# Two stacked transformer blocks with eight experts: the column order of the gate and up products

## The chip, the cores and the metric

The kernel runs on one core of a Trainium2 chip. Its engines work side by side: TensorE multiplies matrices (rows named PE; its loads of the stationary operand are PEld), VectorE (DVE) and ScalarE (ACT) work on elements, GpSimd (POOL) is hardly used, and SyncE (SP) issues most DMA transfers. Data lie in SBUF, 128 partitions wide; TensorE writes its sums to eight banks of PSUM, each with 512 fp32 columns a partition. The metric is device time in microseconds (us) from start to end of one execution, lower is better. Times of single instructions are in nanoseconds (ns).

## What is computed

The reference passes 256 tokens of width 1024 through two blocks. The first has two layers with attention, pooling, a recurrent part and a dense feed-forward part. The second has two layers with convolution and attention; the feed-forward part of its last layer is a mixture of experts. Only that mixture is touched here:

```python
def swiglu(h, w_gate, w_up, w_down):
    return (jax.nn.silu(h @ w_gate) * (h @ w_up)) @ w_down

def moe_swiglu(h, w_router, b_router, w_gate, w_up, w_down):
    ...
    for e in range(N_EXPERTS):          # 8 experts
        out = out + combine[:, e:e + 1] * swiglu(t, w_gate[e], w_up[e], w_down[e])
```

Each token uses its two best experts (`combine` is zero for the others). Gate and up matrices are 1024 x 3584 for each expert, the down matrix is 3584 x 1024, all fp32. All three together are 352 MB, more than half of what the kernel reads.

## The kernel before

**Products in three parts.** An fp32 product is made of rounded parts. ScalarE writes the rounded weights (`whi`, line 1046) from the buffer in which they arrived (`ring`); VectorE subtracts them from the original and writes the rest (`wlo`, in the experts' stage `wlo_moe`, line 1421). For activations the same holds (`xg` is a name of both parts, `xg_hh` and `xg_ht` are the two for the other pair of experts). A product is then hi x hi + hi x lo + lo x hi, three matmuls into the same bank: that is the helper `mm3`, and in the trace all its matmuls of the experts' stage have line 2099. In these matmuls both operands have the type fp32r (rounded). Some small products elsewhere use plain fp32 operands; their stream through TensorE is slower, and the trace shows two records for each such matmul.

**The experts' stage** is written out by hand in `pe_routed`, `act_routed` and `dve_routed`. Tokens of an expert are gathered into 128 places. The loop runs over 56 steps, one for each pair of an expert `e` and a block `f` of 512 of its 3584 hidden columns. A step on TensorE: the gate product (`hidden(n, "gate")`), four transposes of the step before (`turn`, line 2157), the up product, and the down product of the step before. In some steps come small products for gathering and scattering tokens (`gather`, `turn_weights`, `scatter`).

**A gate or up product**: the stationary operand is a 128 x 128 tile of the gathered tokens, the moving operand is a weight tile of 128 x 512, and the result is a whole bank of 128 x 512. Over 8 tiles of the contraction and the three parts this gives 24 matmuls for each. A down product has 24 matmuls too: 4 tiles of the contraction, two banks, three parts, and again 512 moving columns.

**Buffers.** Six slots take the arriving pieces of weights, 1 MB each, six to a step. Each piece is split in two halves of 1024 columns (`HALVES`), for which there are again six places: four in `whi`/`wlo_moe` and two in `EXTRA` (the names `extra_hi`, `extra_lo`). All of them begin at a byte address that is 96 modulo 256 (`WEIGHT_LINE`); the tokens' tiles begin at 32 modulo 256 (`ACT_LINE`). SyncE issues the transfer into a slot when VectorE has read it. Gate products of step n go to bank 0 or 2, up products to bank 1 or 3, from which ScalarE (line 2239, silu) and VectorE (line 2318) read whole rows in the plain order.

Of the kernel before, what the change touches and what calls it, by code (L numbers as in the profile page):

```python
# [124 lines left out]
def build(nc, t, dense=False):  # L125

    with ExitStack() as ctx:
# [55 lines left out]
        def over(name, at, *shape):  # L183
            return nc.alloc_sbuf_tensor_at(name, [128, *shape], F32R, offset=base + 4 * at)
# [5 lines left out]
        XG = [[over(f"xg{i}", 8192 + 2048 * i, 8, 2, 128) for i in range(2)],  # L190
              [nc.alloc_sbuf_tensor_at("xg_hh", [128, 8, 2, 128], F32R, offset=HH_at),
               nc.alloc_sbuf_tensor_at("xg_ht", [128, 8, 2, 128], F32R, offset=hT_at)]]
# [12 lines left out]
        PS = [ctx.enter_context(nc.psum_tensor(f"bank{i}", [128, 512], F32)) for i in range(8)]  # L205
# [1869 lines left out]
        def stage(n):  # L2075

            at = first_moe + 6 * n - (2 if n > 0 else 0)
            up = 2 if n < len(seq) else 0
            return {"gate": range(at, at + up), "up": range(at + up, at + 2 * up),
                    "down": range(at + 2 * up, at + 2 * up + (2 if n > 0 else 0))}  # L2080
# [4 lines left out]
        def pe_routed(pe, tail):  # L2085
# [3 lines left out]
            def take(*name, until):  # L2089
                i = misc[0] % 2  # L2090
                misc[0] += 1
                for signal, *end in misc[1][i]:
                    pe.wait_ge(*signal(*end))
                misc[1][i] = until
                BANK[name] = 6 + i
                return PS[6 + i]

            def mm(out, lhsT, rhs, start, stop):
                return pe.matmul(out, lhsT, rhs, start=start, stop=stop, skip_group_check=True)  # L2099

            def mm3(out, a, b, start, stop):
                mm(out, a[0], b[0], start, False)
                mm(out, a[0], b[1], False, False)
                return mm(out, a[1], b[0], False, stop)

            def half(n, i):
                pe.wait_ge(*(lo_made if n < first_moe + 2 else lambda *x: moe_lo["r"]("lo", *x))(n, i))
                return HALVES[n, i][0:2]

            def gather(p, g, x, bank=None):  # L2110

                until = [(r_vec if x else r_hi, "xg", p, g, x)]
                if bank is None:
                    b = take("xg", p, g, x, until=until)
                else:
                    for signal, *end in tail[bank]:
                        pe.wait_ge(*signal(*end))
                    tail[bank], BANK["xg", p, g, x] = until, bank
                    b = PS[bank]
                pe.wait_ge(*r_vec("select", 2 * p + 1))  # L2120
                for i in range(2):
                    pe.wait_ge(*(v_rout("hnl", i, g // 2) if x else a_rout("hn", i, g // 2)))
                for k in range(2):
                    for i in range(2):
                        at = 128 * (2 * g + k)
                        tm = mm(b[:, S * k:S * k + S], (HNL if x else HNH)[:, i, at:at + 128],
                                PSEL[:, i, 2 * p:2 * p + 2, :].rearrange("p e s -> p (e s)"), i == 0, i == 1)
                tm.then_inc(*r_mm.up(("xg", p, g, x)))
# [8 lines left out]
            def hidden(n, kind):  # L2137
                e = seq[n][0]
                i = 2 * (n % 2) + (kind == "up")
                for signal, *end in ([(r_vec, "hs", n - 2)] if n >= 2 else tail[i]):  # L2140
                    pe.wait_ge(*signal(*end))
                for c, ch in enumerate(stage(n)[kind]):
                    for h in range(2):
                        w = half(ch, h)
                        pe.wait_ge(*r_hi("xg", e // 2, 2 * c + h, 0))
                        pe.wait_ge(*r_vec("xg", e // 2, 2 * c + h, 1))
                        for k in range(2):
                            kk = 4 * c + 2 * h + k
                            tm = mm3(PS[i][:, :], [x[:, kk, e % 2, :] for x in XG[e // 2 % 2]], [x[:, k, :] for x in w],
                                     kk == 0, kk == 7)  # L2150
                        tm.then_inc(*r_w.up(("half", ch, h), (kind, n)))

            def turn(n):
# [39 lines left out]
            for j, (g, x) in enumerate(((0, 0), (1, 0), (0, 1), (1, 1), (2, 0), (3, 0), (2, 1), (3, 1))):  # L2193
                gather(0, g, x, bank=2 + j if j < 4 else None)
            slot_weights(0)
            for n in steps:
                if n < len(seq):
                    hidden(n, "gate")
                if n > 0:
                    turn(n - 1)  # L2200
                if n < len(seq):
                    e, f = seq[n]
                    hidden(n, "up")
                    if n in (1, 3, 5, 7):
                        turn_weights(n - 1)
                    if f in (1, 2) and e > 0:
                        scatter(e - 1, (2 * f - 2, 2 * f - 1))
                    if f >= 3 and e % 2 == 1 and e + 1 < NE:
                        for x in range(2):
                            gather((e + 1) // 2, f - 3, x)  # L2210
                        if f == END:
                            slot_weights((e + 1) // 2)
                if n > 0:
                    down(n - 1)
# [276 lines left out]
        pool_program(Engine(Unissued(), "POOL"))  # L2491
        sp_program(Engine(Unissued(), "SP"))
        pe_routed(pe, tail)
        act_routed(a)
        dve_routed(v)
# [26 lines left out]
        @block.tensor  # L2522
        def _(eng):
            now = Engine(eng, "PE")
            tail = pe_program(now)
            fork(eng, now, lambda pe: pe_routed(pe, tail), lambda pe: pe_everywhere(pe, tail))
# [190 lines left out]
```

## Time and profile before

| | |
|---|---|
| median of 3 runs | 2092.43 us |
| lowest and highest | 2087.53 and 2093.09 us |
| span of the profiled execution, first to last instruction | 2083.4 us |
| median less that span | 9.0 us |
| TensorE busy in the span | 2045.4 us (98%) |
| VectorE, ScalarE busy | 1748.3 us (84%), 1340.7 us (64%) |
| mean granted clock of TensorE | 0.996 |
| experts' stage (first silu to last step) | about 1093 to 2063 us |

The page comes from one execution. Busy time of TensorE is modelled, since its matmuls overlap: the length of a matmul's record is longer than the distance to the next one. What counts for a stretch is the distance between two starts. It is read from the timeline, or from the chain of work, whose pieces name their count of instructions and their time.

### The profile page before, as it was taken

The page shows a single profiled execution, that of the slowest core. Times are in us where ns is not written, and L with a number is a line of the kernel's source. Part 1 is how long each engine was busy: PE and PEld are TensorE (multiplying, and loading weights), DVE is VectorE, ACT ScalarE, POOL GpSimd, SP SyncE. Part 2 cuts the span into 40 slices and gives each one's busy share as a digit, 9 for nine tenths or more (in the row PEclk, how much of TensorE's full clock was granted, in tenths as well). Part 3 has the DMA queues.
Part 4 walks back from the last instruction along what each step waited for, and adds up shares of the span by engine and source line. Part 5 has one row for each costly group of instructions (what it writes and reads, how often), then busy time and mean ns, then how long its engine had stood idle before and what let it go on. Part 6 is the DMA issues. An engine that isn't in the chain of part 4 may idle for free.

```text
span 2083.4 us, 31418 instructions
## 1 busy us (share of the span) xinstructions
PE 2045.4 (98%) x12858; PEld 1801.3 (86%) x12858; DVE 1748.3 (84%) x2215; ACT 1340.7 (64%) x1839; POOL 3.6 (0%) x23
## 2 busy tenths in 40 slices
PE   9999999999999999999989999999999999999998
PEld 8889999889998789999778888888888888888886
DVE  6789886789887867787878998898999889898987
ACT  4655544655545664445667877777777777777775
POOL 0000000000000000000000000000000000000000
PEclk9999999999999999999999999999999999999999
DMA  5357783348784538785449999899998999999994
GB/s 199 132 204 277 258 294 135 143 175 283 253 296 174 173 121 305 254 291 208 145 155 355 365 363 355 341 364 367 359 353 342 366 360 358 349 354 364 363 357 190
DMA packets 94037, 578.03 MB, mean 277 GB/s; under 512 B 11585, under 2 KB 14657, under 8 KB 35649
## 3 DMA queue, kind: packets, MB, share of 16 engines
q1 hardware_dynamic: 92592, 570.03, 73.9%
q0 software_dynamic: 288, 3.15, 0.4%
q10 hardware_dynamic: 1008, 2.80, 0.4%
q8 instruction: 103, 1.69, 0.3%
q14 instruction: 46, 0.37, 0.0%
HBM read 571.75 MB, written 1.05 MB: 275 GB/s over the span
## 4 chain that ended last, share of the span: by engine, by line
PE 87%; DVE 8%; ACT 3%; DMA 1%; issue 1%; DVEq 0%; SPq 0%; ACTq 0%
PE bank L2099 46%; PE bank L513 40%; DVE wlo L1421 2%; PE bank L2157 1%; DVE RSTD L1489 1%; ACT whi L1046 1%; DMA ring<-in_w_in 0%; DVE XC L1454 0%; DMA xT<-in_xT 0%; DVE XC L1498 0%; DVE RSTD L1446 0%; DVE XC L1478 0%; ACT HH L1101 0%; PE bank L946 0%; ACT arena L1176 0%
## 5 line engine op out<-in xcount | busy, mean ns | idle before, releaser
L1046 ACT ACTIVATE whi<-ring 128x1024 fp32r<-128x1024 f32 (+1 forms) x766 | 757.5, 1021 | 154.4 <-PE bank L513 72.6
L1421 DVE TENSOR_TENSOR wlo_moe<-ring,whi 128x1024 fp32r<-128x1024 f32 x448 | 526.1, 1218 | 9.7 <-ACT whi L1046 7.1
L513 PE MATMUL bank<-HH,whi 128*128 128x256 f32 x1536 | 431.0, 281 | 4.3 <-DVE wlo L1421 3.0
L513 PE MATMUL bank<-HL,whi 128*128 128x256 f32 x1536 | 424.3, 276 | 0.0
L513 PE MATMUL bank<-HH,wlo 128*128 128x256 f32 x1536 | 424.3, 276 | 0.0
L1421 DVE TENSOR_TENSOR wlo<-ring,whi 128x1024 fp32r<-128x1024 f32 (+3 forms) x318 | 343.5, 1113 | 80.9 <-ACT whi L1046 80.8
L513 PEld LDWEIGHTS bank<-HH,whi 128*128 128x128 f32 x1536 | 288.4, 188 | 8.6 <-DVE wlo L1421 4.2
L513 PEld LDWEIGHTS bank<-HL,whi 128*128 128x128 f32 x1536 | 288.5, 188 | 0.9 <-issue 0.5
L513 PEld LDWEIGHTS bank<-HH,wlo 128*128 128x128 f32 x1536 | 288.5, 188 | 0.0
L1421 DVE TENSOR_TENSOR extra_lo<-ring,extra_hi 128x1024 fp32r<-128x1024 f32 x224 | 264.2, 1219 | 14.8 <-ACT extra_hi L1046 14.6
L1046 ACT ACTIVATE extra_hi<-ring 128x1024 fp32r<-128x1024 f32 x224 | 229.9, 1061 | 41.1 <-PE bank L2099 41.1
L2099 PE MATMUL bank<-whi,xg 128*128 128x512 f32 x672 | 220.4, 396 | 0.0
L2099 PEld LDWEIGHTS bank<-whi,xg 128*128 128x128 f32 x672 | 126.3, 188 | 27.2
L513 PE MATMUL bank<-midh,whi 128*128 128x256 f32 x528 | 146.6, 278 | 0.3
L513 PE MATMUL bank<-midh,wlo 128*128 128x256 f32 x528 | 145.8, 276 | 0.0
L513 PE MATMUL bank<-midl,whi 128*128 128x256 f32 x528 | 145.8, 276 | 0.0
L2099 PE MATMUL bank<-whi,xg_hh 128*128 128x512 f32 x336 | 134.5, 400 | 0.3 <-DVE wlo_moe L1421 0.3
L2099 PE MATMUL bank<-wlo_moe,xg 128*128 128x512 f32 x336 | 131.7, 392 | 0.0
L2099 PE MATMUL bank<-whi,xg_ht 128*128 128x512 f32 x336 | 131.6, 392 | 0.0
L2099 PE MATMUL bank<-wlo_moe,xg_hh 128*128 128x512 f32 x336 | 131.6, 392 | 0.0
L1529 DVE SCALAR_TENSOR_TENSOR side<-side,cact 128x1024 f32<-128x1024 f32 x84 | 107.5, 1279 | 4.0 <-DMA side<-in_w_ada 3.7
L513 PEld LDWEIGHTS bank<-midh,whi 128*128 128x128 f32 x528 | 99.1, 188 | 0.8 <-DVE wlo L1421 0.7
(296 smaller groups left out, 3486.2 us busy)
## 6 DMA issues: line engine op xcount, KB each, us to landing
ring<-in_moe_gate SPq DMA_DIRECT2D x112, 1024.0 KB, 5.8
ring<-in_moe_up SPq DMA_DIRECT2D x112, 1024.0 KB, 6.7
ring<-in_moe_down SPq DMA_DIRECT2D x112, 1024.0 KB, 5.8
side<-in_w_ada SPq DMA_DIRECT2D x96, 512.0 KB, 4.1
ring<-in_w_up SPq DMA_DIRECT2D x44, 1024.0 KB, 4.9
ring<-in_w_in SPq DMA_DIRECT2D x32, 1024.0 KB, 5.8
ring<-in_w_down SPq DMA_DIRECT2D x32, 704.0 KB, 5.5
ring<-in_ffn_gu SPq DMA_DIRECT2D x22, 1024.0 KB, 4.8
```

The source lines that it names most:

```text
L513: return pe.matmul(out, lhsT, rhs, start=start, stop=stop, skip_group_check=True)
L1046: a.activation(hi, part, ACT.Copy).then_inc(*made.up(("hi", n, i)))
L1421: v.tensor_tensor(lo, part, hi.bitcast(F32), ALU.subtract).then_inc(*done.up(("lo", n, i)))
L1489: v.reciprocal(RSTD[:, 0, :], RSTD[:, 0, :]).then_inc(*v_norm.up((s.name, "rstd")))
L1529: v.scalar_tensor_tensor(at, side_in[n % 2], cact[:, k:k + 1], at, ALU.mult, ALU.add).then_inc(*v_mod.up(("acc", n)))
L2099: return pe.matmul(out, lhsT, rhs, start=start, stop=stop, skip_group_check=True)
L2157: tm = pe.transpose(b[:, 128 * k:128 * k + 128], SGB[n % 2][:, 128 * k:128 * k + 128], ident)
```

## The change

The weight tile of 512 columns and the bank's 512 columns are viewed in another order. With `c=32` and `s=2`, column number 256 s + 32 b + i is visited in the order b (8), then s (2), then i (32): columns 0 to 31, 256 to 287, 32 to 63, 288 to 319, and so on. Operand and result are visited in the same order, so that each result column lands where it did before. The two halves are 256 fp32 columns apart, 1024 bytes. This is done for gate and up products alone, for hi and lo weights alike. No instruction is added, removed or moved on any engine; the 2688 matmuls concerned have access patterns of 8 x 2 x 32 in place of 512.

```diff
@@ pe_routed
+            def woven(x):
+                return x.rearrange("p (s b c) -> p b s c", s=2, c=32)
+
             def gather(p, g, x, bank=None):
...
                         for k in range(2):
                             kk = 4 * c + 2 * h + k
-                            tm = mm3(PS[i][:, :], [x[:, kk, e % 2, :] for x in XG[e // 2 % 2]], [x[:, k, :] for x in w],
-                                     kk == 0, kk == 7)
+                            tm = mm3(woven(PS[i][:, :]), [x[:, kk, e % 2, :] for x in XG[e // 2 % 2]],
+                                     [woven(x[:, k, :]) for x in w], kk == 0, kk == 7)
                         tm.then_inc(*r_w.up(("half", ch, h), (kind, n)))
```

## Rows read from the trace of the kernel before

**Rows 1.** The page: busy time by engine, then the chain's shares

```profile
PE 2045.4 (98%) x12858; PEld 1801.3 (86%) x12858; DVE 1748.3 (84%) x2215; ACT 1340.7 (64%) x1839; POOL 3.6 (0%) x23
...
PE 87%; DVE 8%; ACT 3%; DMA 1%; issue 1%; DVEq 0%; SPq 0%; ACTq 0%
PE bank L2099 46%; PE bank L513 40%; DVE wlo L1421 2%; PE bank L2157 1%; DVE RSTD L1489 1%; ACT whi L1046 1%; DMA ring<-in_w_in 0%; DVE XC L1454 0%; DMA xT<-in_xT 0%; DVE XC L1498 0%; DVE RSTD L1446 0%; DVE XC L1478 0%; ACT HH L1101 0%; PE bank L946 0%; ACT arena L1176 0%
```

**Rows 2.** Waits of PE, 1093 to 2063 us: total, times, longest

```profile
PE bank L2099 <- ACT xg_hh L2226: 0.4, 2, 0.2
PE bank L2099 <- DVE wlo_moe L1421: 0.3, 1, 0.3
PE bank L2099 <- ACT xg L2226: 0.2, 1, 0.2
```

**Rows 3.** Chain in order of time, 1380 to 1480 us: start, us, instructions

```profile
1421.52 0.44 PE bank L2157 x4
1421.96 16.50 PE bank L2099 x72
1438.46 0.44 PE bank L2157 x4
```

**Rows 4.** Timeline, 1438.5 to 1444 us: start us, us, engine, line, instruction

```profile
1439.21 0.39 PE L2099 MATMUL bank<-whi,xg_ht 128*128 128x512 f32 x1
1439.21 0.19 PEld L2099 LDWEIGHTS bank<-whi,xg_hh 128*128 128x128 f32 x1
...
1443.56 0.39 PE L2099 MATMUL bank<-whi,xg_hh 128*128 128x512 f32 x1
```

**Rows 5.** Timeline of PE near 1251 us, then chain, 1240 to 1300 us

```profile
1250.51 0.40 PE L2099 MATMUL bank<-extra_hi,hsh 128*128 128x512 f32 x1
...
1252.61 0.40 PE L2099 MATMUL bank<-whi,hsh 128*128 128x512 f32 x1
...
1261.61 17.66 PE bank L2099 x80
```

**Rows 6.** Timeline of PE, 900 to 901.2 us, the dense stage

```profile
899.78 0.28 PE L513 MATMUL bank<-midh,wlo 128*128 128x256 f32 x1
...
901.14 0.28 PE L513 MATMUL bank<-midh,wlo 128*128 128x256 f32 x1
```

**Rows 7.** Plain fp32: timeline near 11 us, four pieces, contiguous ones

```profile
11.32 0.59 PE L513 MATMUL bank<-XC,cst 128*128 128x256 f32 x2
11.75 0.59 PE L513 MATMUL bank<-SQ,cst 128*128 128x256 f32 x2
...
L513 PE MATMUL bank<-arena x7: 275/592/595, 71.5 to 73.1; 128*128 128x512 f32 x4, 128*128 128x128 f32 x3
...
L513 PE MATMUL bank<-ring,arena 128*128 128x512 f32 x16 | 7.2, 592 | 0.0
```

**Rows 8.** Timeline of PE, 43 to 47.5 us, weight rows of 264 columns

```profile
44.17 0.29 PE L513 MATMUL bank<-whi,HL 128*128 128x264 f32 x1
...
47.49 0.29 PE L513 MATMUL bank<-whi,HL 128*128 128x264 f32 x1
```

**Rows 9.** Groups by form of PE, first and last of ten

```profile
L2099 PE MATMUL bank<-whi,xg 128*128 128x512 f32 x672 | 220.4, 396 | 0.0
...
L2099 PE MATMUL bank<-extra_lo,xg_hh 128*128 128x512 f32 x112 | 43.9, 392 | 0.0
```

**Rows 10.** Busy time by stretch: PE, PEld, DVE, ACT, POOL, clock, DMA, GB/s

```profile
1421.60:1438.50 16.90, 16.90 (x78) 13.87 (x77) 15.13 (x14) 13.22 (x15) 0.00 (x0) 1.00 0.97 359
1243.10:1261.20 18.10, 18.10 (x86) 14.93 (x85) 16.26 (x16) 13.27 (x14) 0.00 (x0) 1.00 0.88 352
1261.20:1279.30 18.10, 18.10 (x86) 14.94 (x85) 15.93 (x15) 13.52 (x15) 0.00 (x0) 1.00 0.91 360
```

**Rows 11.** Splits by form: ACT dense, ACT experts, DVE dense, DVE experts

```profile
L1046 ACT ACTIVATE whi<-ring 128x1024 fp32r<-128x1024 f32 x206 | 210.8, 1051 | 49.4 <-PE bank L513 42.3 <-DMA ring<-in_w_in 6.4
...
L1046 ACT ACTIVATE whi<-ring 128x1024 fp32r<-128x1024 f32 x410 | 421.2, 1060 | 60.9 <-PE bank L2099 56.3
...
L1421 DVE TENSOR_TENSOR wlo<-ring,whi 128x1024 fp32r<-128x1024 f32 x202 | 240.1, 1219 | 47.0 <-ACT whi L1046 47.0
...
L1421 DVE TENSOR_TENSOR wlo_moe<-ring,whi 128x1024 fp32r<-128x1024 f32 x448 | 526.1, 1218 | 9.7 <-ACT whi L1046 7.1
```

## The prediction

> **What bounds the kernel now.** I began with the page: TensorE is busy for 98% of the span, and the chain that ended last lies on it for 87%, of which 46% belong to line 2099, the helper through which all matmuls of the experts go [rows 1]. A busy share says little, since ends of matmuls are modelled, so next came TensorE's own waits between 1093 and 2063 us, the whole experts' stage: three entries, together 0.9 us in 970 [rows 2]. Nothing that TensorE needs comes late there. The chain in order of time says the same in another way: 72 matmuls of line 2099 in 16.50 us, 4 transposes in 0.44 us, and again, without a piece of another engine between them [rows 3]. One step of the experts' loop (one pair of expert and block of 512 columns; there are 56) is 16.94 us, and it is the sum of the distances between starts of its matmuls.
>
> That distance is what the change can touch, so it is the number to read. 16.50/72 gives 229.2 ns. The timeline of the gate matmuls gives it again: 19 starts from 1439.21 to 1443.56 us, 4.35/19 = 228.9 ns [rows 4]. In some steps it is longer: from 1250.51 to 1252.61 us there are nine starts, 2.10/9 = 233.3 ns [rows 5], on the same buffers at the same addresses; the chain there has 80 matmuls (8 short ones of the scatter among them) in 17.66 us. I use 230 ns as the mean of the changed matmuls. The granted clock is 1.00 in all these stretches [rows 10], which is the level of 2.4 GHz, so 512 columns at one a clock would be 213.3 ns. About 16.7 ns of each matmul, 7%, are neither columns nor waits.
>
> **Where these 16.7 ns come from** decides the case, and three comparisons bear on it.
> First, the same engine with unrounded fp32 operands, whose columns come at half the pace: records of 256 columns start 0.43/2 = 215 ns apart [rows 7], against 213.3 for 256 columns at two clocks each. With the slower stream the excess is 2 ns. So the excess belongs to operands that move at one column a clock.
> Second, in the dense stage the rounded matmuls of 256 columns start 1.36/12 = 113.3 ns apart [rows 6], against 106.7 ns of columns: 6.7 ns on 256. On 512 that would be 226.7; the experts' matmuls show 2.5 to 6.6 ns more than this.
> Third, the matmuls of 264 columns, whose weight rows lie 1056 bytes apart, start 3.32/27 = 123.0 ns apart [rows 8], where 264 columns at the dense rate are 116.9 ns: 6.1 ns more for no work. Together with the two levels of the experts' step this says that at one column a clock the distance depends on how reads meet, on place or phase. An edit that changes nothing but the order of addresses can therefore move it, in either direction.
>
> **The change part by part.** Every product of gate and up has the weights as its moving operand, 512 columns. The change views these columns, and the columns of the bank that takes the result, as 8 x 2 x 32: 32 columns of the first half, 32 of the second, 1024 bytes further, the next 32 of the first. Number, order, operands, waits and signals of all instructions stay. There are 8 x 3 matmuls for gate and as many for up, 48 a step, 2688 in all; ten groups by form add up to that, of which the first and the last stand in [rows 9]. The third of the stage's matmuls that makes up the down products is untouched, and so is everything before the stage.
> Nothing is hidden: TensorE has no idle time there, so one nanosecond on each of the 2688 is 2.69 us of the kernel, gain or loss. The units:
> - Upper end of a gain: the distance falls from 230 to the 215 of the slower stream: 15 x 2688 = 40 us.
> - No effect: 0.
> - Loss: 15 more jumps in the read and 15 in the write. For jumps alone the trace has mild rows. ScalarE takes 1051 ns for its split when it reads 8 pieces of 128 columns (dense stage) and 1060 ns when it reads 1024 in a row; VectorE takes 1219 and 1218 ns [rows 11]. TensorE itself has, for the two matmuls of line 753 (unrounded operands), four records of 512 columns that read four pieces of 128 columns, 1024 bytes apart: 592 to 595 ns, against 592 for sixteen contiguous ones [rows 7]. But all of these move slower than a column per 2.4 GHz clock, and would hide a bubble that the experts' matmuls would show. The nearest row at full rate is the 264-column one. Its 6.1 ns, taken once for each matmul, are 16 us; taken once for the read and once for the write they are 33 us.
>
> Between -40 and +33 us I choose a gain of half the excess, 7.5 ns: 7.5 x 2688 = 20 us. My reason is the geometry. Beside each matmul runs the weight load of the next one [rows 4]. In the dense stage each matmul has such a load of 128 columns of its own and they start 113.3 ns apart, so the load needs at most 272 clocks, about two a column. Now the moving stream runs through 256 bytes in 64 clocks, twice as fast as the loading one, and catches it again and again. Woven, with the two halves a multiple of 256 bytes apart, it comes forward by 256 bytes in 128 clocks, the pace of the load. If the excess is two streams meeting on the same part of memory, they would meet less. This is an inference from the two levels and the 264-column rows, not something a row shows.
>
> **What is late next.** If a step shrinks, the others must keep pace. VectorE is busy 15.13 of 16.90 us in a fast step, ScalarE 13.22 [rows 10]; a step of 16.94 - 48 x 0.0075 = 16.58 us leaves both room. The DMA engines are busy 0.97 of that step: 16.4 us of transfers. So a fast step can't fall by more than about 0.5 us; the longer steps, with a share of 0.88 to 0.91, have 1.6 to 2 us. The forecast of 0.36 us a step fits. The full gain of 0.72 us would not in the fast steps: with some 37 of the 56 steps cut at 0.5 us the most is 37 x 0.5 + 19 x 0.72 = 32 us.
>
> [...]
>
> **Rivals.**
> - *Jumps cost* (slower). At full rate each of the jumps, read or write, leaves a bubble that the slower rows hide. Price 6.1 to 12.2 ns, 16 to 33 us: 2109 to 2125 us. It decides as soon as the mean distance of gate and up is above 232.3 ns. For it: no slack at all in this stage, and a 7% excess which shows that the supply of operands is at its limit already. Against: the jump rows of three engines.
> - *The order is indifferent* (same). The excess is a fixed toll for each 256 columns (6.7 ns dense, 13.3 of the 16.7 here), the rest is phase, and neither cares about the order of pieces. 2092 us, within 6. For it: 6.7 ns are there in the dense stage whatever is read. Against: 264 columns.
> - *Full gain, then the DMAs* (faster): 32 us, 2060 us.
> - That the change doesn't do what it says can be ruled out: the view gives 8 x 2 x 32 on operand and bank alike.
>
> **How the numbers follow.** The profiled execution has a span of 2083.4 us; the median of the three runs is 2092.4, 9.0 more, which lie before the first and after the last instruction and don't change. 2083.4 - 20 + 9 = 2072 us. Chances: gain by part or all of the excess 0.42 (of it the full one 0.10), indifferent 0.25, jumps cost 0.33 (of it 0.10 beyond 33 us). A measurement tells about 0.3%, 6 us, from no change. The range goes from 2058, just under the DMA limit, to 2125, the double price of the jumps; outside are the dear end of the jumps and a little below.
>
> **What would show it.** Right: chain pieces of 72 matmuls of 16.1 to 16.2 us in place of 16.50, distances of about 221 ns for gate and up with 229 kept for down, DMA share near 0.99. Indifferent: 16.50 again. Jumps: distances above 235 for gate and up alone, the down ones as before, and the DMA share down. The forecast is wrong if the distance of the changed matmuls does not fall, and its reason is wrong if it falls but doesn't depend on the size of the pieces.

## The result: 18 us slower

| | before | after |
|---|---|---|
| median | 2089.98 us (4 runs beside those of after) | 2108.15 us (4 runs) |
| lowest and highest | 2087.27 and 2093.09 us | 2105.52 and 2112.45 us |
| span of the profiled execution | 2083.4 us | 2106.0 us |
| mean distance of the 2688 gate and up matmuls | 229.7 ns | 236.6 ns |
| mean distance of the 1344 down matmuls | 230.3 ns | 229.4 ns |

The ratio is 1.0086, with a 95% interval from 1.0068 to 1.0104. A distance is that between the starts of two matmuls that follow each other, as in the prediction; the means are taken over all start times of the experts' stage, without the first matmul after another kind of work (where TensorE changes over, some 320 ns). The mean before was 229.7 ns, where the prediction used 230. Ratios further down are to the kernel before, measured beside the run in question, with the 95% interval in brackets; where one run is named, there is a single time and no interval. Such a time says less than the distances do: four kernels that share the distance of 229.7 ns (the one before and three of those below) also share the time from the first to the last expert matmul, 984.7 to 984.8 us, while their spans go from 2083.4 to 2091.1 us.

**The profile after.** These rows of the page answer to [rows 1]; the chain's shares and the counts of instructions are as they were, and TensorE's busy time is 22 us longer:

```profile
PE 2067.8 (98%) x12858; PEld 1805.5 (86%) x12858; DVE 1751.9 (83%) x2215; ACT 1340.8 (64%) x1839; POOL 3.6 (0%) x23
...
PE 87%; DVE 8%; ACT 3%; DMA 1%; issue 1%; DVEq 0%; SPq 0%; ACTq 0%
```

TensorE's waits over the experts' stage (1099 to 2080 us), as [rows 2]:

```profile
PE bank L2099 <- ACT xg_hh L2229: 0.4, 2, 0.2
PE bank L2099 <- ACT xg L2229: 0.2, 1, 0.2
```

So no wait took the place of anything: 0.6 us in 981. The matmuls themselves stand further apart. The chain in order of time, as [rows 3] (a fast step), then as the last of [rows 5]:

```profile
1433.67 16.86 PE bank L2099 x72
```

```profile
1270.91 17.81 PE bank L2099 x80
```

Both steps with 80 matmuls hold eight short ones that gather tokens (`psel`, from 1266.95 us before and 1276.43 us after), not the scatter that the prediction named; a scatter step has eight short ones too and takes as long.

And the timeline of one gate product, as [rows 4], and of a down product, as the first two of [rows 5]:

```profile
1433.97 0.40 PE L2099 MATMUL bank<-whi,xg_ht 128*128 128x512 f32 x1
...
1438.94 0.40 PE L2099 MATMUL bank<-whi,xg_ht 128*128 128x512 f32 x1
```

```profile
1261.89 0.39 PE L2099 MATMUL bank<-whi,hsh 128*128 128x512 f32 x1
...
1264.63 0.40 PE L2099 MATMUL bank<-whi,xg 128*128 128x512 f32 x1
```

The first pair holds 21 distances: 4.97/21 = 236.7 ns for gate, against 228.9 before. The second holds 12: 2.74/12 = 228.3 ns for down. Down products are not changed, yet in such a step, one with a scatter, they stood 233.3 ns apart before. The slower of the two levels is gone, and a fast step has grown by 0.36 us (16.50 to 16.86), a step with eight short matmuls more by 0.15 us only (17.66 to 17.81).

The sum: gate and up 2688 x 6.85 ns = 18.4 us more, down 1344 x 0.84 ns = 1.1 us less, together 17.3 us. The stage itself shows it. Its first expert matmul starts at 1088.05 us before and at 1093.87 us after, and the spans end at 2083.4 and 2106.0, so the stage took 995.4 and 1012.1 us: 16.8 us more. The other 5.8 us of the difference between the spans came before any changed instruction, and belong to these two executions, not to the change. TensorE's granted clock has the size for it: its mean over the span was 0.996 before and 0.993 after (some 6 us of 2083, an estimate), and 1.00 in the stage in both.

```profile
1088.05 0.48 PE L2099 MATMUL bank<-whi,xg 128*128 128x512 f32 x1
```

(timeline of before), and in that of after

```profile
1093.87 0.48 PE L2099 MATMUL bank<-whi,xg 128*128 128x512 f32 x1
```

VectorE and the DMA engines followed, as the windows of one fast step show (columns as in [rows 10]): the DMA share is 0.93 where it was 0.97.

```profile
1416.00:1433.30 17.30, 17.30 (x79) 13.93 (x78) 15.25 (x14) 13.25 (x15) 0.00 (x0) 1.00 0.93 368
```

### The profile page after: what moved, and what is told of

It is laid out like the page before. It is cut to its first block, busy times and chain, and to the rows that moved or that the text cites. A ratio compares the mean times of both kernels' runs of the same rounds, so it can differ in the third digit from the quotient of the medians.

```text
span 2106.0 us, 31418 instructions
## 1 busy us (share of the span) xinstructions
PE 2067.8 (98%) x12858; PEld 1805.5 (86%) x12858; DVE 1751.9 (83%) x2215; ACT 1340.8 (64%) x1839; POOL 3.6 (0%) x23
## 4 chain that ended last, share of the span: by engine, by line
PE 87%; DVE 8%; ACT 3%; DMA 1%; issue 1%; DVEq 0%; SPq 0%; ACTq 0%
PE bank L2099 46%; PE bank L513 40%; DVE wlo L1421 2%; PE bank L2160 1%; DVE RSTD L1489 1%; ACT whi L1046 1%; DMA ring<-in_w_in 0%; DVE XC L1454 0%; DMA xT<-in_xT 0%; DVE XC L1498 0%; DVE RSTD L1446 0%; DVE XC L1478 0%; ACT HH L1101 0%; PE bank L946 0%; ACT arena L1176 0%
## 5 line engine op out<-in xcount | busy, mean ns | idle before, releaser
L1421 DVE TENSOR_TENSOR wlo_moe<-ring,whi 128x1024 fp32r<-128x1024 f32 x448 | 529.1, 1220 | 13.9 <-ACT whi L1046 8.8
L2313 DVE TENSOR_TENSOR hsl<-bank,hsh 128x512 fp32r<-128x512 f32 x56 | 38.7, 692 | 77.4 <-ACT hsh L2247 76.7
```

The costliest lines, as they stand in the source:

```text
L1421: v.tensor_tensor(lo, part, hi.bitcast(F32), ALU.subtract).then_inc(*done.up(("lo", n, i)))
L2313: v.tensor_tensor(lo, PS[BANK["turn", n - 1]][:, :], hi.bitcast(F32), ALU.subtract).then_inc(*r_vec.up(("hst", n - 1)))
```

## Is it the read or the write?

The first theory after the result was the rival of the prediction, in two forms: R, jumps of the read cost; W, jumps of the write to PSUM cost. One kernel weaves only the weights, one only the bank. In each the columns of the hidden units are in the wrong order.

```diff
-                            tm = mm3(woven(PS[i][:, :]), ...
+                            tm = mm3(PS[i][:, :], ...
```

> Only the weights (moving operand) are read in the woven order; the bank is written in plain order, so the expert columns are permuted and the result is not the reference's. The changed kernel has 236.6 ns between starts of gate and up matmuls, the kernel before 229 to 231. Theory R, a jump of the read costs: about 236.6 ns again, 2108 us. Theory W, a jump of the write to PSUM costs: 229 to 231 ns, 2090 us. If both share the cost, about 233 ns.

Measured: 2107.37 us, ratio 1.0081 (1.0059 to 1.0102); gate and up 236.6 ns.

```profile
1430.62 16.86 PE bank L2099 x72
```

```diff
-                                     [woven(x[:, k, :]) for x in w], kk == 0, kk == 7)
+                                     [x[:, k, :] for x in w], kk == 0, kk == 7)
```

> Only the bank is written in the woven order; the weights are read in plain order, so the result is not the reference's. Theory R: 229 to 231 ns between starts, 2090 us. Theory W: 236.6 ns, 2108 us.

Measured: 2090.37 us, ratio 0.9989 (0.9978 to 0.9999); gate and up 229.7 ns.

```profile
1429.64 16.50 PE bank L2099 x72
```

All of the cost is in the read (16.86 us a step again), and the woven write is free at full rate. The Trainium skill says that any non-contiguous access pattern in PSUM slows matmuls significantly (page PSUM - Partial Sum Buffer, section Specifications). The trace does not agree: sixteen pieces of 32 columns in PSUM leave the distance at 229.7 ns. The Trainium skill also says that every two consecutive elements should be contiguous (page Advanced Engine Details and Errata, section PSUM Cachelines). The pieces of 32 meet that, and no run here goes against it.

## Does each jump cost?

Two kernels change the size of the pieces and nothing else; both have the reference's result.

```diff
-                return x.rearrange("p (s b c) -> p b s c", s=2, c=32)
+                return x.rearrange("p (s b c) -> p b s c", s=2, c=16)
```

> The whole change with pieces of 16 columns in place of 32: 32 pieces a matmul in place of 16. If each piece costs the same (7.4 ns / 16 = 0.46 ns, about one clock of 2.4 GHz), 229.2 + 14.8 = 244 ns between starts of gate and up, 56 x 48 x 7.4 ns = 20 us more than the changed kernel, 2128 us. If the cost comes once for each matmul, 236.6 ns and 2108 us. If it comes from how the moving stream meets the weight load (the pace of both is 256 bytes in 128 clocks in either case), 236.6 ns as well.

Measured: 2120.14 us (one run), gate and up 240.0 ns.

```profile
1438.32 17.02 PE bank L2099 x72
```

> The whole change with pieces of 64 columns (256 bytes): 8 pieces a matmul. If each piece costs one clock: 229.2 + 3.7 = 233 ns, 2099 us. If the cost comes once for each matmul, 236.6 ns. If the pace against the weight load matters, something else than on this line between 229 and 237.

Measured: 2090.93 us (one run), gate and up 229.7 ns.

```profile
1427.48 16.50 PE bank L2099 x72
```

A clock for each piece would have given 233 ns with 8 pieces and 244 with 32. It gave 229.7 and 240.0. Eight jumps are entirely free: even the steps in which down products stand 233 ns apart in place of 229 are as many as in the plain order, 16 of 56. So the jumps are not what costs. The difference is in where they lead. A piece of 64 columns is 256 bytes, and the other half of the row is 1024 bytes on. Taken modulo 256 the read with such pieces walks exactly as the plain one. With pieces of 32 it walks over 128 bytes, goes back, and walks over them again. That is a new theory, the line theory, and it could be set against jumps directly: 16 pieces of 32 columns, all more than 32 columns apart, with the walk of the plain order modulo 256.

```diff
-                return x.rearrange("p (s b c) -> p b s c", s=2, c=32)
+                first = x[:, 0:32]
+                return bass.AP(first.tensor, first.offset, [first.ap[0], [64, 4], [96, 4], [1, 32]])
```

> Writes in plain order, reads 16 pieces of 32 columns, at columns 0, 96, 192, 288, then the same from column 64, 128 and 192 on: some columns are read twice and others never, so the result is not the reference's. Jump theory (a jump between pieces of 32 columns costs about 0.46 ns, whatever its distance): 236.6 ns between starts of gate and up, about 2108 us. Line theory (what counts is the address modulo 256 bytes, and this walk has 0, 128, 0, 128 bytes and so the same as a plain one): 229.7 ns, 2090 us.

Measured: 2092.52 us (one run), gate and up 229.7 ns.

```profile
1429.18 16.50 PE bank L2099 x72
```

The other way round, all even pieces of 32 and then all odd ones; the read stays for half a matmul on one 128 of every 256 bytes:

```diff
-                return x.rearrange("p (s b c) -> p b s c", s=2, c=32)
+                return x.rearrange("p (b s c) -> p s b c", s=2, c=32)
```

> Read and write both take the even pieces of 32 columns first and then the odd ones; the result is the reference's. As many pieces as in the changed kernel. Jump theory: 236.6 ns, 2108 us. Line theory: the read stays for 256 columns on the same 128 of every 256 bytes and then on the other 128, so the distance leaves 236.6 ns; if coming back to the same bytes too soon is what costs, it is above 240 ns, over 2117 us.

Measured: 2107.63 us (one run), gate and up 236.6 ns.

```profile
1431.67 16.87 PE bank L2099 x72
```

The first falls on the line theory to a tenth of a nanosecond. The second misses the number written for it (above 240 ns): staying longer on the same half costs no more than going back once, as the woven order does. What the two have in common is that a piece of 32 columns is followed by another one on the same 128 bytes, every time here and every second time in the woven order.

These runs also fix the 256. Modulo 128 bytes the plain, the woven and these last two walks are all the same, and they have two different distances; modulo 512 the walks with pieces of 64 and with pieces at 0, 96, 192 and 288 are not the plain one, and they cost nothing.

If pace mattered, a read that runs through the 256 bytes faster should be better. Every second piece of 16 columns, then the others:

```diff
-                return x.rearrange("p (s b c) -> p b s c", s=2, c=32)
+                return x.rearrange("p (b s c) -> p s b c", s=2, c=16)
```

> Read and write take every second piece of 16 columns first, then the others; the result is the reference's. 32 pieces of 64 bytes, and the read comes forward by 256 bytes in 32 clocks, where the plain one needs 64 and the woven one 128. If the toll falls with the pace of the moving stream (woven 236.6, plain 229.7): below 229 ns, down to 226.5, and 2082 us. If only every second line of 64 bytes in use is a kind of staying: 236 to 240 ns, 2108 to 2118 us.

Measured: 2120.05 us, ratio 1.0141 (1.0113 to 1.0169), gate and up 240.1 ns, and a fast step of the chain has 17.01 us.

```profile
1404.31 17.01 PE bank L2099 x72
```

Pace is out: this read comes forward by 256 bytes in 32 clocks and is as dear as pieces of 16 in the woven order, at half the plain pace. It uses 128 of the 256 bytes for half a matmul, as many as the order with even and odd pieces of 32, and costs 3.5 ns more than that one. So the number of bytes in use is not all that counts either: with pieces of 16 the distance is 240 ns in both orders, with pieces of 32 it is 236.6 ns in both.

## Does the weight load meet it?

The prediction's reason was that the weight load of the next matmul hinders the moving read. Theory P says so, theory Q says that the moving read hinders itself. The first pair moves the weights' buffers from 96 to 160 modulo 256:

```diff
-WEIGHT_LINE = 96
+WEIGHT_LINE = 160
```

> The kernel before with the weight buffers at 160 modulo 256 in place of 96, so 128 bytes after the tokens' tiles in place of 64. Theory P, the moving stream meets the weight load of the next matmul (tokens' tiles at 32): the distance of gate and up changes by some ns from 229.7. Theory Q, the moving stream hinders itself: 229.7 ns and 2090 us. The dense stage (distance 113.3 ns) reads the tokens as the moving operand and has the weights as the stationary one: P expects a change there as well, Q none.

Measured: 2120.22 us, ratio 1.0132 (1.0107 to 1.0157); gate and up 232.4 ns, down 232.6, and the dense stage 116.7 ns in place of 113.6 on 6192 matmuls. Timeline of the dense stage:

```profile
919.80 0.28 PE L513 MATMUL bank<-midl,whi 128*128 128x256 f32 x1
...
921.88 0.28 PE L513 MATMUL bank<-midl,whi 128*128 128x256 f32 x1
```

18 distances in 2.08 us are 115.6 ns in this stretch, where [rows 6] had 113.3.

The woven order with the same places:

> The changed kernel with the weight buffers at 160 modulo 256. P: woven, the moving stream goes at the pace of the weight load, and with 128 bytes between them it stays on the other half, so the toll falls, to below 229 ns and below 2090 us. Q: 236.6 ns and 2108 us as at 96.

Measured: 2126.61 us, ratio 1.0165 (1.0141 to 1.0190); gate and up 236.7 ns.

In the dense stage the moving operand is the tokens', which did not move; the stationary one moved for `whi`, while `wlo` stayed at 224. So a place modulo 256 matters beyond that of the moving read, which Q denied. That it is the load which feels it is not shown: between the starts of (`HL`, `whi`) and (`HH`, `wlo`), where neither operand nor the next load moved, the distance rose from 113.8 to 117.1 ns as well, and ScalarE's writes and VectorE's reads of `whi` moved with the buffer. No run separates these. The woven order did not fall below 229 ns, as P had promised with numbers; it stayed at 236.7, and its gap to the plain order is 4.3 ns here because the plain one got dearer.

The second pair lets the load stand still: it reads one token column 128 times.

```diff
-[x[:, kk, e % 2, :] for x in XG[e // 2 % 2]]
+[x[:, kk, e % 2, 0:1].broadcast_to([128, 128]) for x in XG[e // 2 % 2]]
```

> The kernel before, but the weight loads of gate and up read one column of the tokens' tile 128 times in place of 128 columns, so the load moves over no other bytes (the result is not the reference's). P (the moving stream meets the weight load): the distance of gate and up changes, and falls towards 215 ns if meetings are the whole excess, 2052 us. Q (the moving stream hinders itself): 229.7 ns as before.

Measured: 2099.39 us (one run), gate and up 231.6 ns.

> The same with the woven read and write. P: the 6.9 ns between woven and plain go away or change, since there is no walking load to be met; the two kernels of this pair show the same distance. Q: 236.6 ns, the same 6.9 ns above its pair.

Measured: 2095.86 us (one run), gate and up 234.0 ns.

```profile
1432.53 16.61 PE bank L2099 x72
```

(plain) and

```profile
1425.91 16.75 PE bank L2099 x72
```

(woven). Both expectations missed on both sides: the plain order got dearer by 1.9 ns, the woven one cheaper by 2.6. The gap of 6.9 ns shrinks to 2.5, so some 4 ns of the woven toll hang on the load walking beside it, and some don't. The bulk of what the plain order has above its columns (16 ns) doesn't go away when the load stands still. The two times lie the other way round than the distances, since the first expert matmul starts at 1096.84 us in the first execution and at 1088.36 us in the second; from the first to the last expert matmul they take 990.0 and 994.9 us.

The third pair moves the load of gate and up by 64 bytes, to the same place modulo 256 as the weights, and leaves all else (16 columns of the tokens' tile are wrong ones):

```diff
-[x[:, kk, e % 2, :] for x in XG[e // 2 % 2]]
+[bass.AP(x[:, kk, e % 2, 0:1].tensor, x[:, kk, e % 2, 0:1].offset + (16 if kk < 7 else -16),
+         [x[:, kk, e % 2, 0:1].ap[0], [1, 128]]) for x in XG[e // 2 % 2]]
```

> The kernel before, but the weight loads of gate and up begin 16 columns (64 bytes) later in the tokens' tiles, at the same place modulo 256 as the moving rows (16 wrong columns, so the result is not the reference's). The dense stage and down are untouched. P: gate and up leave 229.7 ns, by 2 to 7 ns. Q: 229.7 ns.

Measured: 2084.95 us (one run), gate and up 229.1 ns, down 229.2 ns with no step at 233.

```profile
1406.73 16.50 PE bank L2099 x72
```

A fast step is as long as before. What went is the slower level of some steps.

> The changed kernel (read and write woven), with the weight loads of gate and up 64 bytes further on as in the plain one above (16 wrong columns). Plain it gave 229.1 ns in place of 229.7. If the woven toll comes from how the woven read lies to the load: another distance than 236.6 ns, lower if 64 bytes were the unlucky place. If the woven read hinders itself: 236.6 ns.

Measured: 2111.51 us (one run), gate and up 236.6 ns.

Again the plain order feels the place of the load a little and the woven one doesn't.

## Where the 13 ns come from

Next the moving read itself stood still, on one weight column read 512 times, with the load on one column as well, first 64 bytes apart modulo 256 and then at the same place:

```diff
-[x[:, kk, e % 2, :] for x in XG[e // 2 % 2]], [x[:, k, :] for x in w],
+[x[:, kk, e % 2, 0:1].broadcast_to([128, 128]) for x in XG[e // 2 % 2]],
+[x[:, k, 0:1].broadcast_to([128, 512]) for x in w],
```

> The kernel before, but gate and up read one column of the weights 512 times and their weight load one column of the tokens 128 times, 64 bytes apart modulo 256 (96 and 32); the result is not the reference's. If the excess of 13.3 ns that all kernels share comes from addresses (lines that change), it goes: about 215 ns between starts, about 2050 us. If it is a toll for each column read at the full pace, whatever the address: 226.7 ns, 2081 us.

Measured: 2057.74 us (one run), gate and up 215.8 ns.

> The same, but both fixed columns at the same place modulo 256 (96 and 96). If two reads at the same place modulo 256 hinder each other (the meeting theory), this pair is clearly slower than the pair 64 bytes apart, by more than the 6.9 ns of the woven order. If not, both show the same distance, and meetings modulo 256 are out as the cause.

Measured: 2049.16 us (one run), gate and up 215.8 ns.

```profile
1402.04 0.38 PE L2099 MATMUL bank<-whi,xg_ht 128*128 128x512 f32 x1
...
1406.57 0.38 PE L2099 MATMUL bank<-whi,xg_ht 128*128 128x512 f32 x1
```

(apart; 21 distances in 4.53 us, 215.7 ns). Of the 16.4 ns above 213.3 only 2.5 are left, at the same full rate and with as many columns: the other 13.9 are no toll on the rate, they belong to the addresses that the moving read walks over. Whether two standing reads lie at the same place makes no difference; the times differ by 8.6 us, but from the first to the last expert matmul both take 947.4 to 947.7 us.

The Trainium skill (page TensorE: Matmul & The Clock Gate, section Back-to-back issue gap) gives N/2.4 + 2.5 ns at the full clock as the gap of an isolated matmul, 215.8 ns for 512 columns, and about 131 ns for each matmul of 512 columns in a stream of weight loads and matmuls. The first number is what this stream shows where the moving read stands still; with fp32r columns that are all different it shows 229.7 ns. No run here comes near 131 ns.

Last, how many bytes the moving read goes over again and again. Each kernel does two sizes, one for gate and one for up, with the load walking as usual:

```diff
+            def narrow(x, kind):
+                c = {"gate": 1, "up": 8}[kind]
+                if c == 1:
+                    return x[:, 0:1].broadcast_to([128, 512])
+                return x[:, 0:c].unsqueeze(1).broadcast_to([128, 512 // c, c])
```

> The kernel before; gate reads one weight column 512 times, up reads 8 columns (32 bytes) 64 times, and the weight load walks over its 128 columns as usual (the result is not the reference's). With the load standing still too, one column gave 215.8 ns. If a walking load hinders a standing read (meeting): gate is above 218 ns. If only the walk of the moving read makes the toll: gate 215.8 ns. Up: 215.8 ns if 32 bytes count as one line, more if coming back to the same bytes costs.

Measured: 2052.34 us (one run); gate (1 column) 215.8 ns, up (8 columns) 216.0 ns.

```profile
1412.28 0.38 PE L2099 MATMUL bank<-wlo_moe,xg_hh 128*128 128x512 f32 x1
...
1417.24 0.39 PE L2099 MATMUL bank<-extra_hi,hsh 128*128 128x512 f32 x1
```

(an up product with 8 columns: 23 distances in 4.96 us, 215.7 ns)

> The same with gate on 32 columns (128 bytes) 16 times and up on 16 columns (64 bytes) 32 times. The order far_order stayed on 128 of every 256 bytes and gave 236.6 ns, as the woven order. If staying modulo 256 is what costs: gate 236.6 ns, and up 240 ns as with pieces of 16. If the toll comes from fetching new lines and not from their place modulo 256: both well under 229 ns.

Measured: 2113.68 us (one run); gate (32 columns) 236.7 ns, up (16 columns) 241.2 ns.

```profile
1411.88 0.40 PE L2099 MATMUL bank<-whi,xg_hh 128*128 128x512 f32 x1
...
1417.32 0.41 PE L2099 MATMUL bank<-extra_hi,xg_ht 128*128 128x512 f32 x1
...
1418.24 0.41 PE L2099 MATMUL bank<-wlo_moe,xg_hh 128*128 128x512 f32 x1
...
1423.59 0.41 PE L2099 MATMUL bank<-whi,xg_ht 128*128 128x512 f32 x1
```

(gate: 23 distances in 5.44 us; then up: 22 in 5.35 us, 243.2 ns in this step)

That is the clearest series of the study. By the bytes that the moving read uses before it comes round:

| bytes | kernel | distance | above 213.3 ns |
|---|---|---|---|
| 4 | narrow, 1 column | 215.8 ns | 2.5 |
| 32 | narrow, 8 columns | 216.0 ns | 2.7 |
| 64 | narrow, 16 columns | 241.2 ns | 27.9 |
| 64 twice, then the next 64 twice | pieces of 16 | 240.0 ns | 26.7 |
| two pieces of 64, 128 apart, then the other two | every second piece of 16 | 240.1 ns | 26.8 |
| 128 | narrow, 32 columns | 236.7 ns | 23.4 |
| 128, then the other 128 | the change; even, then odd pieces of 32 | 236.6 ns | 23.3 |
| all 256 (plain walk) | before; pieces of 64; 16 pieces in the plain walk | 229.7 ns | 16.4 |

The changed kernel lies on this line: it costs what it costs to go round in 128 bytes, and it fetches 512 different columns where the narrow one fetches 32. New data cost nothing, the walk modulo 256 bytes does. Eight columns, 32 bytes, are nearly free (0.2 ns more than one column). Above that, the narrow reads are the dearer the less they go over: spread over the 64 steps of 32 bytes in a matmul it is (241.2 - 215.8)/64 = 0.40 ns with 64 bytes in use, 0.33 with 128 and 0.22 with all 256. The orders with pieces of 16 show that bytes in use are not the full rule: one of them uses 128 bytes and costs 0.38. The mean of 241.2 ns has two levels as well, of 55 up products 34 at 240 ns, the level of the other orders with pieces of 16, and 21 at 243 ns.

One rival is untested. All these rows start at 96 modulo 256, so 8 columns lie within one aligned 64 bytes, 16 columns reach over a multiple of 128, and each piece of 16 or 32 crosses multiples of 64. Whether 8 columns are cheap for their size or for their place, no run tells; a narrow read from another start would.

## A version that beats both kernels

The shifted load had pointed at a better place. This kernel has the plain order and the reference's result; the weights of the experts' stage, hi and lo, lie at 32 modulo 256, as the tokens' tiles do, and the dense stage keeps its places.

```diff
-        wlo_moe = nc.alloc_sbuf_tensor_at("wlo_moe", [128, NHALF, HALF], F32R, offset=wlo_at - LOW_LINE + WEIGHT_LINE)
+        wlo_moe = nc.alloc_sbuf_tensor_at("wlo_moe", [128, NHALF, HALF], F32R, offset=wlo_at - LOW_LINE + ACT_LINE)
+        whi_moe = nc.alloc_sbuf_tensor_at("whi_moe", [128, NHALF, HALF], F32R, offset=whi_at - WEIGHT_LINE + ACT_LINE)
...
-            return at_ + (WEIGHT_LINE - at_) % 256
+            return at_ + (ACT_LINE - at_) % 256
...
-                           for x, y in ((whi, EXTRA[0]), (wlo if n < first_moe else wlo_moe, EXTRA[1])))
+                           for x, y in ((whi if n < first_moe else whi_moe, EXTRA[0]), (wlo if n < first_moe else wlo_moe, EXTRA[1])))
```

> A proper kernel with the reference's result: the order of the kernel before, and the weight buffers of the experts' stage at 32 modulo 256 in place of 96, so at the same place as the tokens' tiles, for gate, up and down. In the run with the shifted load gate and up went from 229.7 to 229.1 ns and down from 230.3 to 229.2, since the level of 233 ns in some steps was gone: together 3 us. Expected: 3 us less than the kernel before, 0 to 6; down now lies in the same way and may move by some ns either way. If VectorE or ScalarE meet new hindrance, nothing changes, since neither is late.

Measured: 2081.96 us (9 runs) against 2091.47, ratio 0.9959 (0.9947 to 0.9971). Gate and up 227.5 ns, down 227.3 ns.

```profile
1425.38 16.37 PE bank L2101 x72
```

```profile
1266.91 17.34 PE bank L2101 x80
```

The second chain piece had 17.66 us in [rows 5]: the level of 233 ns is gone. Here the fast step is shorter too, 16.37 us in place of 16.50, which it was not with the shifted load. 2688 x 2.2 + 1344 x 3.0 ns are 9.9 us, and the medians give 9.5. The expectation (3 us, at most 6) was too small: it took over 0.6 and 1.1 ns from the run with the shifted load, and it became 2.2 for gate and up and 3.0 for down. Which of the moved reads and writes of these buffers gave that is not shown. The DMA share of a stretch is 0.97 here. That leaves a little: the kernels with standing reads, at 0.98, had fast steps of 16.3 to 16.4 us, where this one has 16.8:

```profile
1400.00:1500.00 100.00, 100.00 (x461) 83.06 (x461) 91.07 (x87) 78.97 (x85) 0.00 (x0) 1.00 0.97 370
```

## Why the prediction was wrong

- **What bounds the stage: right.** TensorE waited for 0.9 us before and for 0.6 after; 1 ns on 2688 matmuls is 2.69 us, and 6.85 ns came to 18 us. In the kernels with standing reads the stage followed TensorE down to 215.8 ns with a DMA share of 0.98, so the limit by the DMAs (0.5 us a fast step) was drawn a little too tight: a fast step (the 72 matmuls of the chain's row and the 0.44 us beside them) fell there from 16.94 to 16.4 and 16.3 us.
- **The excess belongs to the full rate and depends on the place of reads: right, and it went further.** Standing still on one column removes all of it but 2.5 ns. The comparison with unrounded operands (215 ns) had the lower bound right.
- **The choice between the ends: wrong.** The failed step is that, since the woven read goes at the pace of the weight load, the two streams "would meet less", which was to give back 7.5 ns. It took a ratio of paces for the cause. Measured, the woven read costs 6.9 ns more; another pace (the kernel with every second piece of 16) costs 10.4 more; and with a load that doesn't walk the woven order is still 2.5 ns dearer than the plain one. What the runs showed in its place is that the walk of the moving read modulo 256 bytes brings the toll, and that the change made it go back over the same 128 bytes. The load has a part in it: 4 of the 6.9 ns are there only when it walks too. That part has the opposite sign of the forecast: the walking load makes the woven order dearer against the plain one, not cheaper.
- **The rival "jumps cost": its time was right, its mechanism wrong.** It had 2109 us for a single price of 6.1 ns; measured were 2108 and 6.85 ns. But 16 jumps in the same walk cost nothing, and 8 jumps cost nothing. The 6.1 ns of the 264-column matmuls [rows 8] hit the size by luck or by kinship: those rows start at another place modulo 256 each time. No run tells which.
- **"The order is indifferent": wrong** for the read, right for the write.
- **The forecast for the down matmuls (229 kept): right on the whole, incomplete.** Unchanged instructions behind changed ones lost the level of 233 ns in some steps, which gave back 1.1 us.
- **The 9.0 us between span and median** were said to lie outside of the first and last instruction. The changed kernel's profiled execution took 2108.01 us with a span of 2106.0: only 2 us lie outside. The rest was that the profiled execution of before was a quick one, with a mean granted clock of 0.996.

What could have been seen beforehand: nothing in the trace of before showed a read in another walk at full rate, so the sign was open. With chances of 0.42 and 0.33 that was said; the point forecast should then have leaned less on a reason that no row bore.

**What stays open.** Why a narrower walk costs more. That places of 32 bytes need some time before they can be read again would fit the narrow series, but not the pieces of 16 taken every second time: they come back to a place after 32 columns, as the even and odd pieces of 32 do, and cost 240.1 against 236.6 ns. The part of the load (4 of the 6.9 ns, and the places at 32, 96 and 160) isn't explained by it either. That the standing reads didn't care for each other speaks against a simple meeting of the two. The two levels of 229 and 233 ns on the same addresses are open too.

## What to carry to other kernels

Where TensorE has no idle time, read the distance between starts of its matmuls and compare it with columns over clock; a per cent of it is a per cent of the stage. In this kernel a pattern in pieces of 32 columns was free on the write, and pieces were free on the read as long as the walk modulo 256 bytes stayed the plain one (pieces of 64 fp32 columns, or jumps that continue at the next place); a read that goes back over the same 64 or 128 bytes cost 3 to 5%. Try the places of both operands modulo 256 before the order: that was worth 0.4% here, and the wrong place cost 1.3%.

## What the runs showed of the hardware

- fp32r matmuls with a walking moving operand start 229.7 ns apart at 512 columns (227.5 at a better place), and 215.8 ns apart when it stands still, at a granted clock of 1.00 in both.
- A moving read of 8 columns over and over costs 0.2 ns more than one column (216.0 ns); 16 columns are the dearest of those tried (241.2 ns). All began at 96 modulo 256.
- A read in 8 or 16 pieces costs nothing (229.7 ns) if its walk modulo 256 bytes is the plain one, and 6.9 ns more if it goes back over the same 128 bytes; a write to PSUM in 16 pieces costs nothing.
- The Trainium skill (page TensorE: Matmul & The Clock Gate, first step of the section Step-by-step: what each phase is for) says that loading the next weights takes no SBUF read bandwidth from the running matmul. The trace agrees for the most part, since with a standing load the plain distance is 231.6 ns, no shorter than the 229.7 with a walking one; but a standing load takes the gap between woven and plain from 6.9 to 2.5 ns, so the two reads are not quite independent.
- Weights at 160 in place of 96 modulo 256 made the kernel 1.3% slower: 113.6 to 116.7 ns in the dense stage, 229.7 to 232.4 for gate and up. Which of the accesses to these buffers feels it is not shown.
- The distance of unchanged matmuls can move with the access pattern of their neighbours: in some steps the down matmuls stood 233 ns apart before and 229 ns apart behind woven gate and up products.
